# The small steps of an mLSTM and forgetting-attention layer moved to other places between its dense units

## The reference, cut to what matters

```
h      = rmsnorm(x);  proj = h @ w_in        # mo mk mq mv | ga gb | fk fq fv, and a few gates
h_a    = mlstm(q, k, v, gates, C0, n0, m0)   # 4 heads of 256; prompt in 2 chunks of 128 tokens
h_a    = sigmoid(mo) * rmsnorm(h_a);         branch_a = h_a @ w_branch_mlstm     # "bm"
o_b    = forgetting_attention(rmsnorm(fq), rmsnorm(fk), fv, past keys and values)
branch_b = o_b @ w_branch_fox                                                    # "bf"
x      = x + (sigmoid(ga)*branch_a + sigmoid(gb)*branch_b) @ w_out               # "out"
x      = x + moe(rmsnorm(x))                 # 32 experts, top 1 group, top 2 experts
```

## Time and profile before

| | |
|---|---|
| median of 3 runs | 906.62 us (901.59 to 908.42) |
| the profiled execution's own time | 908.45 us |
| its span | 907.0 us |
| PE busy | 763.5 us (84%) |
| DVE, ACT, POOL busy | 401.9, 300.8, 144.4 us |
| chain that ended last | PE 54%, DMA 17%, DVE 13%, ACT 8%, issue 6% |
| granted TensorE clock, mean | 0.934 of 2.4 GHz |

### The profile page before, as it was taken

The page is one execution under the profiler, slowest core; times in us unless marked ns, Lnnn a source line. Parts: engine busy times, 40 slices in busy tenths (PEclk is TensorE's granted clock), DMA queues, the critical chain, the costliest instruction groups (busy, mean ns, idle before and its releaser), DMA issues.

```text
span 907.0 us, 14392 instructions
## 1 busy us (share of the span) xinstructions
PE 763.5 (84%) x5476; PEld 605.1 (67%) x5476; DVE 401.9 (44%) x936; ACT 300.8 (33%) x552; POOL 144.4 (16%) x245
## 2 busy tenths in 40 slices
PE   2999999977799898999778898989399999787780
PEld 1788999965456588999666678988274555444440
DVE  3574334454345443657455545773753222111113
ACT  5434354533323343556222224443421111111110
POOL 5001000002134200011231310000302222222210
PEclk9999999987789989999998989999699999999996
DMA  5233433223568615273575551893849999999985
GB/s 177 95 139 132 142 139 134 94 78 132 151 190 243 207 41 186 94 250 132 191 247 158 169 183 54 333 352 142 327 167 418 417 418 418 420 419 419 417 335 184
DMA packets 38170, 202.84 MB, mean 224 GB/s; under 512 B 7490, under 2 KB 8018, under 8 KB 18898
## 3 DMA queue, kind: packets, MB, share of 16 engines
q1 hardware_dynamic: 24434, 160.29, 46.0%
q0 software_dynamic: 13664, 41.58, 14.4%
HBM read 184.24 MB, written 23.38 MB: 229 GB/s over the span
## 4 chain that ended last, share of the span: by engine, by line
PE 54%; DMA 17%; DVE 13%; ACT 8%; issue 6%; POOL 0%; POOLq 0%; SPq 0%; DVEq 0%; ACTq 0%
PE bank L1677 18%; DMA fm<-in_w_moe 9%; PE bank L1681 7%; PE bank L2020 6%; DVE rm L1089 3%; PE bank L1832 3%; DMA em<-in_w_moe 3%; ACT rm L773 3%; PE bank L2040 3%; PE bank L1667 3%; PE bank L1881 2%; PE bank L1916 2%; PE bank L2001 1%; DMA fm<-in_cache_lf 1%; PE bank L1821 1%
## 5 line engine op out<-in xcount | busy, mean ns | idle before, releaser
L1677 PE MATMUL bank<-rm 128*128 128x320 f32 x1344 | 211.4, 317 | 2.4 <-issue 1.6
L1677 PEld LDWEIGHTS bank<-rm 128*128 128x128 f32 x1344 | 202.7, 193 | 7.7 <-issue 6.1
L1089 DVE TENSOR_TENSOR rm<-fm,rm 128x2048 fp32r<-128x2048 f32 x48 | 110.1, 2293 | 83.5 <-ACT rm L773 83.0
L1681 PE MATMUL bank<-rm 128*128 128x256 f32 x960 | 126.5, 292 | 7.2 <-DVE rm L1089 3.6
L1681 PEld LDWEIGHTS bank<-rm 128*128 128x128 f32 x960 | 122.1, 199 | 8.4 <-DVE rm L1089 3.8
L773 ACT ACTIVATE rm<-fm 128x2048 fp32r<-128x2048 f32 x48 | 91.9, 1915 | 25.7 <-PE bank L1677 16.9
L2022 PE MATMUL bank<-fm,em 128*64 128x256 f32 x384 | 96.6, 397 | 0.0
L2020 PE MATMUL bank<-em 128*64 128x256 f32 x272 | 68.1, 395 | 9.6 <-DMA fm<-in_w_moe 4.8
L2020 PE MATMUL bank<-fm,em 128*64 128x256 f32 x240 | 60.3, 397 | 12.6 <-DMA fm<-in_w_moe 11.3
L2020 PEld LDWEIGHTS bank<-em 128*64 128x64 f32 x272 | 36.2, 141 | 36.8 <-issue 22.1
L1052 ACT ACTIVATE fm<-bank 64x256 f32<-64x256 f32 x32 | 12.0, 376 | 136.5 <-PE bank L2022 136.5
(11 more groups left out here) (388 smaller groups left out, 1032.8 us busy)
## 6 DMA issues: line engine op xcount, KB each, us to landing
fm<-in_w_moe SPq DMA_DIRECT2D x57, 1024.0 KB, 26.6
fm<-in_w_dense SPq DMA_DIRECT2D x48, 1024.0 KB, 4.9
em<-in_w_moe SPq DMA_DIRECT2D x39, 1024.0 KB, 26.1
fm<-in_state_C POOLq DMA_DIRECT2D x32, 257.0 KB, 4.2
out_C_sample<-fm POOLq DMA_DIRECT2D x32, 257.0 KB, 5.3
fm<-in_cache_kT POOLq DMA_DIRECT2D x16, 512.0 KB, 5.0
fm<-in_cache_v POOLq DMA_DIRECT2D x16, 512.0 KB, 4.5
fm<-y_rows SPq DMA_DIRECT2D x4, 512.0 KB, 5.1
```

Of the source, the lines that this page charges most:

```text
L1089: s(TT(pair[c % 2][1], cube(raw[c % RAW1], KC), pair[c % 2][0], ALU.subtract), sem("split_done"))
L1677: ins = mm(bank[b][:, 0:NT], w[:, k, P * u:P * (u + 1)], a[:, k, :], start=first, stop=final)
L1681: ins = mm(bank[b][0:r, 0:CW], a[:, k, TILE0[u]:TILE0[u] + r], w[:, k, :], start=first, stop=final)
```

## The change

- The five G steps stand three units apart instead of two (behind units 2, 5, 8, 11, 14 instead of 1, 3, 5, 7, 9).
- F1 is cut in two: F1 (squares and variance) and F3 (root and scaling). For tile 0 they stand behind units 36 and 37 with F2 behind 38; for tile 1 behind 42 and 43 with F2 behind 44 (before: F1 behind 41, F2 behind 43); for the samples behind 52 and 53 with F2 behind 55 (before: 50 and 52).
- The P2 steps of the second prompt chunk begin one unit later and SB two units later (behind 43 to 51, nine units, instead of 41 to 50, ten units).
- Two `Cout` buffers move to where `W` of the prompt tiles lay, so ACT waits for the stores only at the first unit of fq; at the first unit of fk it waits for `cout_full`, DVE's last SB.
- SP's wait ahead of the two small loads becomes `num_full` and stands two chunks later.
- The first chunk of `out` is done in two passes: slices 0 to 5 of all three units, then slices 6 and 7 of all three. The first unit of bf waits for its input slice by slice.

```diff
     for n in range(1, 6):
-        after("mo", 0, 1, 2 * (n - 1)).append(("G", n, 0))
+        after("mo", 0, 1, 1 + 3 * (n - 1)).append(("G", n, 0))
...
     after("ga", 0, 0).append(("F1", 0, 0))
+    for h in range(HM):
+        after("ga", 1, 1, h).append(("P2", 1, h))
+        after("ga", 0, 1, h).append(("P1", 1, h))
+    after("ga", 0, 1).append(("F3", 0, 0))
     after("ga", 1, 0).append(("F2", 0, 0))
...
-            line = after("ga", 2, 1, (h * BS + b) * 10 // (HM * BS))
+            line = after("ga", 3, 1, (h * BS + b) * 9 // (HM * BS))
...
-                if c == first("fk") + 1:
-
-                    sp.wait_ge(sem("ha_split"), 6)
+                if c == first("fk") + 3:
+
+                    sp.wait_ge(sem("num_full"), 3 * HM)
...
                 if sec == "fk" and cc == 0 and u == 0:
+
+                    act.wait_ge(sem("cout_full"), HM * BS)
+                if sec == "fq" and cc == 0 and u == 0:
 
                     act.wait_ge(sem("stored"), 16 * 5)
...
                 s(A_(small[0:r, 24:28], small[0:r, 20:24], ACT.Copy), sem("num_squared"))
+
+            def F3(st):
+                t = st[1]
+                r = ROWS[t]
                 act.wait_ge(sem("num_var"), t + 1)
                 s(A_(small[0:r, 36:40], small[0:r, 32:36], ACT.Sqrt), sem("num_rooted"))
...
-                if u == 0 and sec == "bf" and cc == 0:
-                    pe.wait_ge(sem("o_split"), KC)
...
+                    if u == 0 and sec == "bf" and cc == 0:
+                        pe.wait_ge(sem("o_split"), k + 1)
...
+                if c == first("out"):
+
+                    for u in range(3):
+                        dense(c, u, range(KC - 2))
                 for u in range(units_of(c)):
-                    dense(c, u)
+                    dense(c, u, range(KC - 2, KC) if c == first("out") else range(KC))
```

More of the change, by code:

```diff
@@ L237, in hybrid_step @@
         Cin = [cube(take(2 * DE), 2) for _ in range(3)]
-        at = base_gb + KC * NT + 2 * DE * (NCOUT - 2)
+        at = base_gb + KC * NT
         Cin.append(cube(fm[:, at:at + 2 * DE], 2))
         assert at + 2 * DE <= base_gb + 2 * D + 2 * HM * DE
-        Cout = [cube(take(2 * DE), 2) for _ in range(2)] + \
-            [cube(fm[:, base_gb + KC * NT + 2 * DE * i:base_gb + KC * NT + 2 * DE * (i + 1)], 2) for i in range(NCOUT - 2)]
+        Cout = [cube(take(2 * DE), 2) for _ in range(2)]
         W = take(3 * HM * P).rearrange("p (t h s) -> p t h s", t=3, h=HM)
+        W_two, W_one, W_zero = W[:, 0], W[:, 1], W[:, 2]
+        W = [W_zero, W_one, W_two]
+        take(2 * 2 * DE - 2 * HM * P)
+        for i in range(2):
+            at = top[0] - 2 * DE * (2 - i)
+            Cout.append(cube(fm[:, at:at + 2 * DE], 2))
         base_num = top[0]
@@ L1220, in P1 @@
                     pe_past(("P2", (n - 2) // HM, (n - 2) % HM))
-                done(TT(SW[n % 2], bank[3][:, 0:128], W[:, c, h, :], ALU.mult), 3)
+                done(TT(SW[n % 2], bank[3][:, 0:128], W[c][:, h, :], ALU.mult), 3)
             def P2(st):
@@ L1279, in SA @@
                 pe_past(("P2", 1, HM - 2 + h) if h < 2 else ("SB", h - 2, BS - 1))
-                done(TT(SW[n % 2][0:NS, 0:64], bank[3][0:NS, 0:64], W[0:NS, 2, h, 0:64], ALU.mult), 3)
+                done(TT(SW[n % 2][0:NS, 0:64], bank[3][0:NS, 0:64], W[2][0:NS, h, 0:64], ALU.mult), 3)
                 if h == 0:
@@ L1637, in full, with dense @@
                 ins.then_inc(sem(f"bank_full{b}"), 1)
-            def dense(c, u):
+            def dense(c, u, ks=range(KC)):
                 sec, cc = SECTIONS[c // CPS], c % CPS
@@ L1660, in dense @@
                 b = (n0 + u) % NRING
-                if u == 2:
-                    for s in ("samp_hi", "samp_lo"):
-                        pe.wait_ge(sem(s), 1 if sec != "out" else 1 + KC)
-                    for k in range(KC):
+                for k in ks:
+                    if u == 2:
+                        for s in ("samp_hi", "samp_lo"):
+                            pe.wait_ge(sem(s), 1 if sec != "out" else 2 + k)
                         for i, w in enumerate((hi, lo)):
```

35 lines of the change are left out of this document (18 added, 17 removed).

## The result

The changed kernel took **876.19 us** (median of 4 runs, 872.82 to 883.48), the kernel before 907.52 beside it: ratio 0.968, 95% interval 0.963 to 0.973. On another chip it took 875.49 (6 runs, 873.76 to 877.71) against 904.64, ratio 0.967 (0.963 to 0.971). The profiled execution took 872.89 us, its span is 871.4, mean clock 0.949. PE is busy for 750.2 us instead of 763.5, with the same matmuls.

The account below looks back on a forecast made before the run. The prediction took PE's path ahead of the sort, plus a fixed expert stream, as the bound. Terms 2 + 16.5 + 10.2 + 1.6 + 1.5 = 31.8 off 908.45 gave 876.7, 876 for the median; range 867 to 884, with rivals 866 to 890.

Parts of the forecast that it names:

- The end follows the sort: Tail: the end is the sort's end plus a fixed expert stream, so time saved on PE before it counts one for one.
- Gates, 2: Gate steps three units apart: two stalls go, the third grows to 2.4, clock returns 1.3; gain about 2 us, bounds 0 and 4.6.
- Units 38 to 51, 16.5: Moved steps in units 38 to 51: 11.1 us of stalls net plus 5.5 of clock, bounds 11 and 22.
- fk, 10.2: First fk chunks: waits of 1.97 and 3.61 go, plus 4.6 of clock; gain 10.2 us, lower bound 7.
- bf, 1.6: Start of bf: the wait of 1.59 becomes one by slices that DVE finishes faster than PE reaches them; gain 1.6 us.
- out, 1.5: First chunk of `out`: two passes fill PE's 2.86 wait, but a later wait of about 2 comes; gain 1.5 us, bounds 0 and 4.8.
- the first (clock stays low, 886): Rival: short waits in runs of SB steps hold the clock down, only stalls are gained, 20.4 us, 886; chance 0.12.
- The second (state blocks): Rival: state loads and stores land too late in runs of SB steps, gain falls by 10 to 15, 886 to 891; chance 0.09.
- The third: Rival: the expert stream, not PE, sets the start of the tail, so nothing changes, 906; chance 0.04.
- The fourth: Rival: the 3.6 stall behind F2 of tile 1 lowers the clock, not recovering before fk; slower, 916; chance 0.03.

Follow-up runs that it names:

- SP's wait moved: Kernel before with only SP's wait changed to DVE's last SB and placed two chunks later: 895.85 us against 903.1, ratio 0.993.
- one pass: Changed kernel with the first chunk of `out` done in one pass again: 876.88 us against 875.49 for the changed kernel on the same chip.
- waits of chosen length: Changed kernel with PE held behind units 15, 18, 21 and 24 for 2, 4, 6 and 8 small POOL writes: 889.66 us in one execution.
- old places: Changed kernel with the steps behind units 36 to 52 back in the places of the kernel before: 898.76 us, ratio 0.992.
- F1 and F3 ahead: Changed kernel with F1 and F3 of prompt tile 1 joined ahead of the first SB again: 885.19 us, ratio 0.979.
- the gates back: Changed kernel with the five gate steps two units apart again: 880.37 us, ratio 0.974.
- better SB schedule: Changed kernel with four SB steps per unit, F2 of tile 1 behind unit 44's: 867.12 us; with later gate steps and earlier `out` preparation too, 863.43.

## Why the prediction was right

The forecast was 876 us, with 31.8 us of gain. The medians gave 876.19 and 875.49, which is 31.3 and 29.2 under the kernel before beside them, and the two pairs of spans 32.2 on average. The mechanism was right in its main terms: taking single moves back, or making one alone, showed their waits come and go nearly as counted. That the sum came so close is partly luck: the largest term varies by several us from execution to execution, and one loss that was not in the sum and one small term with a wrong step were made up by others. Term by term:

- **The end follows the sort.** Right: 250 us from the sort to the end in both kernels, and the sort ended at 635.5 and 637.0 us where near 640 was forecast.
- **Gates, 2.** Right, 2.6 by the ledger, 2.7 to 2.9 by undoing it. The makeup was off: I counted 2.4 for one wait, and there are two, 1.58 for ACT's evacuation and 1.03 for the split behind it (in the second profile the clock was lower in between, and the second wait is not there). The 1.3 of clock in my sum was worth only 0.4, since without it PE waits 0.86 at the next step.
- **Units 38 to 51, 16.5.** Right: 17.6, with 16.4 to 18.8 between the single pairs. The waits of the stretch from KT to fk fell from 24.9 to 13.0, 11.9 against my 11.1. One was too small: 4.08 where I had 3.6; of the waits of 0.44 there are seven, not eight; the two at the heads came as counted. The clock gave the remainder, 4.2 to 6.9 in these two pairs against my 5.5. But two other kernels with the old steps here and two others with the new ones put it lower (table below): over four executions of each order the stretch gains 15.2, 12.0 of waits and 3.2 of clock. So the waits were sized right, and the clock's term was on the high side.
- **fk, 10.2.** Right, 10.5: 6.4 for SP's wait and 4.1 for F2. (F1 and F3 of the samples stand one unit apart, not two as I wrote; no wait came of it.) SP's is the smallest edit with the largest effect for its size. From the order of the work it is also a precondition: with F2 of the samples behind the third chunk's split, a wait for F2's result ahead of that chunk's load would never end. This was not run.
- **bf, 1.6.** Right, 1.8.
- **out, 1.5.** Wrong in a step, though small in the sum. The wait of some 2 us ahead of the second chunk came as counted (2.36), but I put nothing for the clock behind it, and it cost 1.5 in every profile of the changed order (some 4.6 for 3.1). The 0.9 in the ledger is waiting saved; the clock lost about as much behind the new wait as before behind the old one. On the other side I counted the drop behind the old wait as certain. It came in both profiles of the kernel before and in neither of the two others that have the same wait (SP's wait moved, and one pass), where the stretch takes 61.84 and 61.86, no more than the 61.97 of the two passes. So the edit is worth between 0 and 1 us.
- **What the sum lacked.** Between the fourth chunk of fk and the end of bm the changed kernels lose 2 to 3 us: nine of the ten profiles of kernels made from the changed one show 202.1 to 203.5, and three made from the one before 198.5, 200.5 and 201.3. It does not lie where ACT's wait for the stores went: the first eight chunks of the stretch, from fk's fourth to fv's third, take 67.70 us instead of 68.98, and ACT waits there for no store. It lies behind them, in the last chunk of fv and in bm, where the attention steps are: 134.6 and 135.0 us instead of 132.3 and 129.5. The waits of the whole stretch are 23.5 to 25.1 and 22.6 to 24.0, so about one us of the loss is waits and the rest clock. The tenth profile, the one with waits of chosen length, has the changed code there and took 200.6. So at least part of it is scatter of the clock; what brings the rest stays open. The start of the program, 1.0 us in our favour, is nothing that the change touched.

Of the rivals, the first (clock stays low, 886) is refuted where the SB steps with their waits of 0.44 and 0.17 follow each other. From 231 to 256 us, which holds two runs with these waits and the units behind them, the granted clock is 1.00, and the units take 3.78:

```profile
231.00:256.00 25.00, 21.12 (x128) 13.58 (x128) 10.92 (x32) 10.75 (x19) 8.68 (x16) 1.00 0.77 219
```

The page "TensorE: Matmul & The Clock Gate" of the Trainium skill, section "A second HAM failure mode: psum-queue depth-cycling", tells of a bf16 kernel whose clock swings because PE idles shortly between groups of matmuls that cycle through banks. In this trace such idles alone did not bring the clock down (four matmuls in 0.70, the next unit in 3.78). The second (state blocks) is refuted too: the DMA share rose to 0.73, and no row of PE in the stretch waits for a transfer; with four steps to each of eight units there is one wait of 0.3 us. The third falls with the ledger. The fourth needed a clock that does not recover behind 4.08; it was back 6 us behind the end of that wait in one profile and 11 us in the other.

For the ledger's third row, here are the waits against what is left when they are taken out (KT to fk, us):

| kernel | stretch | waits | rest |
|---|---|---|---|
| before, twice | 210.9, 210.7 | 24.9, 25.3 | 186.0, 185.3 |
| SP's wait alone | 208.1 | 24.8 | 183.2 |
| old places | 208.0 | 25.0 | 183.0 |
| F1 and F3 ahead | 202.4 | 18.3 | 184.1 |
| changed, four executions (one with `out` in one pass, one with the gates back) | 192.1, 194.2, 195.2, 195.4 | 13.0 each | 179.1, 181.2, 182.2, 182.4 |
| better SB schedule, twice | 185.4, 184.9 | 7.2, 7.0 | 178.2, 177.9 |

PE's instructions are the same in all, so the differences in the last column are the clock: its mean over the stretch is 0.92 in both executions of the kernel before, 0.94 in the next two rows, 0.93 with F1 and F3 ahead, 0.95 to 0.96 in the changed order and 0.97 in the better one. The waits of the changed order repeat to a hundredth, those of the old one to 0.4 us; the clock's share moves by about 3 us between executions of one order.

## What to carry to other kernels

Put a small step's parts on different engines a full dense unit apart, and look for what the *other* engine must do first: one root with its table load ahead of 0.8 us of keys cost 8 us. Look in the DMA queue for waits that stand ahead of loads they have nothing to do with. A wait removed pays for itself and often for time at the lower clock (1.5 to 2.6 us behind chosen waits of 2.45 to 4.77, 1.8 to 4.8 behind 4.08, 0 to 1.3 behind 2.86), but only where no second wait stands behind it. Where a new wait comes, price the clock behind it too. Ask what is late next, as with DVE's preparation in `out`, before splitting a loop to fill a hole.

## What was not expected of the hardware

- What the clock does is not fixed by the program. Behind one and the same wait of 1.13 to 1.14 us two units took 8.84 or 7.31 in two executions of the kernel before (and 8.84 with the gates back). Behind 4.07 to 4.08 the loss fell on the first matmuls or a unit later, in two executions of the changed kernel. Behind 2.85 to 2.86, 30 matmuls took 5.53 and 5.22 in the kernel before and 4.26 in two other kernels with the same wait; behind 2.36 the drop came eight times in eight. One profile shows that a drop can occur, not its mean price.
- It goes with the scatter of the runs: of the first four runs of the changed kernel the two shortest, 872.82 and 872.89 us, had mean clocks of 0.955 and 0.949, the longest, 883.48, one of 0.941. One stretch of 190 us accounts for about 3 of these us; the others were not followed up.
- 26 matmuls in place of an idle 4.08 us kept the clock at its upper level, at no cost in time (one execution): the next SB step began 9.31 us after the dense unit's start with them and without.
